# Small experts that add their row sums before the activation, a later transpose in the split experts, and norms that take their statistics from other operations

## What is computed

```python
def hier_moe(...):                      # first block, 32 experts of hidden width 256, 2 per token
    hg = silu(x @ w_gate[e]) * (x @ w_up[e])
    y += (hg * weight) @ w_down[e]
x = layer_norm(DN_ALPHA * x + y, ln2_g[layer], ln2_b[layer])

def second_block(x, ...):
    h = rmsnorm(x, norm_mix_w[l])       # l = 0 follows the last layer_norm above at once
    x = x + hybrid_mixer(h, ...)
    ...
    x = x + moe_swiglu(h, ...)          # second layer: 8 experts of hidden width 2816, 2 per token
```

## Time and profile before

| | |
|---|---|
| time, median of 3 runs (lowest, highest) | 2469.22 us (2465.05, 2471.34) |
| profiled execution: its time, and its span | 2465.34 us, 2463.3 us |
| mean granted TensorE clock | 0.983 of full |
| busy: PE, DVE, ACT | 94%, 72%, 56% of the span |
| weight traffic by SP's queue | 590.84 MB |

### The profile page before, as it was taken

How to read it: one execution, slowest core, us unless ns; L and a number is a source line. 1 busy time by engine, 2 the same in 40 slices (tenths; PEclk the granted TensorE clock), 3 DMA queues, 4 the chain that set the end, 5 groups by cost and what they waited for, 6 DMA issues and landing times.

```text
span 2463.3 us, 39708 instructions
## 1 busy us (share of the span) xinstructions
PE 2308.1 (94%) x14770; PEld 2068.1 (84%) x14770; DVE 1780.3 (72%) x2016; ACT 1378.1 (56%) x1522; POOL 70.2 (3%) x122
## 2 busy tenths in 40 slices
PE   7889999998899999988999998889999999999997
PEld 6789999877799998977899897778788887788876
DVE  5577775646777775885566688558888888888886
ACT  4455654445455653464433346437777777777775
POOL 0100000101000002000000200000000000000000
PEclk9999999999999999999999999989999999999999
DMA  7349999631399995634355652319899999998993
GB/s 266 127 151 364 366 374 327 171 107 51 113 359 375 376 353 127 211 101 135 120 181 170 160 183 91 132 36 361 324 331 390 337 357 374 329 390 330 338 394 116
DMA packets 253818, 609.51 MB, mean 247 GB/s; under 512 B 11217, under 2 KB 103201, under 8 KB 229009
## 3 DMA queue, kind: packets, MB, share of 16 engines
q1 hardware_dynamic: 247776, 590.84, 66.1%
q0 software_dynamic: 5248, 13.25, 2.4%
q10 hardware_dynamic: 560, 2.10, 0.2%
HBM read 605.11 MB, written 1.05 MB: 246 GB/s over the span
## 4 chain that ended last, share of the span: by engine, by line
PE 76%; DVE 13%; ACT 5%; issue 3%; DVEq 2%; DMA 1%; ACTq 0%; POOLq 0%
PE psum L137 15%; PE psum L139 15%; PE psum L138 15%; PE psum L2332 10%; PE psum L2368 9%; PE psum L2356 2%; DVE weight_ring_rounded L116 2%; DVE h_cf L3229 1%; ACT weights_high_rounded L2066 1%; PE psum L936 1%; ACT scores L970 1%; PE psum L2885 1%; PE psum L2015 1%; DVE weight_ring_rounded L2071 1%; PE psum L621 1%
## 5 line engine op out<-in xcount | busy, mean ns | idle before, releaser
L2071 DVE TENSOR_TENSOR weight_ring_rounded<-weight_ring,weights_high_rounded 128x2048 fp32r<-128x2048 f32 x264 | 603.7, 2291 | 101.5 <-ACT weights_high_rounded L2066 101.4
L2066 ACT ACTIVATE weights_high_rounded<-weight_ring 128x2048 fp32r<-128x2048 f32 x264 | 504.9, 1917 | 157.3 <-PE psum L139 142.9
L2429 DVE TENSOR_TENSOR weight_ring_rounded<-weight_ring,weights_high_rounded 128x2048 fp32r<-128x2048 f32 x128 | 293.0, 2292 | 96.8 <-ACT weights_high_rounded L2424 96.8
L137 PE MATMUL psum<-weights_high_rounded,scores_rounded 128*128 128x512 f32 (+1 forms) x768 | 291.2, 379 | 8.6 <-DVE weight_ring_rounded L2071 4.5
L139 PE MATMUL psum<-weights_high_rounded,scores_rounded 128*128 128x512 f32 (+1 forms) x768 | 287.0, 374 | 0.0
L138 PE MATMUL psum<-weight_ring_rounded,scores_rounded 128*128 128x512 f32 (+1 forms) x768 | 286.3, 373 | 0.0
L2332 PE MATMUL psum<-weights_high_rounded,scores_rounded 128*128 128x256 f32 x1024 | 262.6, 294 | 5.6 <-issue 3.3
L139 PE MATMUL psum<-weights_high_rounded,xT_rounded 128*128 128x512 f32 (+3 forms) x688 | 259.6, 377 | 0.0
L2332 PE MATMUL psum<-weight_ring_rounded,scores_rounded 128*128 128x256 f32 x1024 | 252.4, 284 | 0.0
L2368 PE MATMUL psum<-xT_high,weight_ring 128*128 128x128 f32 x2048 | 240.4, 276 | 7.3 <-DVE xT_high L2500 4.0
L2424 ACT ACTIVATE weights_high_rounded<-weight_ring 128x2048 fp32r<-128x2048 f32 x128 | 244.3, 1908 | 0.0
(11 more groups left out here) (580 smaller groups left out, 4123.5 us busy)
## 6 DMA issues: line engine op xcount, KB each, us to landing
weight_ring<-in_moe_w_gate_dram SPq DMA_DIRECT2D x152, 1024.0 KB, 6.0
weight_ring<-in_moe_w_up_dram SPq DMA_DIRECT2D x152, 1024.0 KB, 8.4
weight_ring<-in_moe_w_down_dram SPq DMA_DIRECT2D x152, 1024.0 KB, 8.3
weight_ring<-in_w_in_dram SPq DMA_DIRECT2D x20, 1024.0 KB, 7.2
weight_ring<-in_ffn_w_gate_dram SPq DMA_DIRECT2D x11, 1024.0 KB, 5.3
weight_ring<-in_ffn_w_up_dram SPq DMA_DIRECT2D x11, 1024.0 KB, 5.4
weight_ring<-in_ffn_w_down_dram SPq DMA_DIRECT2D x11, 1024.0 KB, 4.9
weight_ring<-in_w_out_dram SPq DMA_DIRECT2D x8, 1024.0 KB, 5.1
```

Of the source, the lines that this page charges most:

```text
L137: nc.tensor.matmul(out, lh, rh, start=start, stop=False)
L2066: self.c.nc.scalar.activation(ring.high(self.s0 + q, 1, SLOT), ring.view(self.p0 + q, 1, SLOT), ACT.Copy).then_inc(ring.high_ready, 1)
L2071: self.c.nc.vector.tensor_tensor(ring.low(self.p0 + q, 1, SLOT), ring.view(self.p0 + q, 1, SLOT), ring.high(self.s0 + q, 1, SLOT).bitcast( ...
L2429: self.c.nc.vector.tensor_tensor(ring.low(tile, 1, SLOT), ring.view(tile, 1, SLOT), ring.high(s, 1, SLOT).bitcast(F32), ALU.subtract).then ...
```

## The change

Four parts.

1. `SmallExperts`. ScalarE copies only the 64 low rows from PSUM, VectorE adds them to the 64 high rows, ScalarE takes the Silu of the sums (64x256), and VectorE multiplies (64x256), all in row form. TensorE then transposes the finished hidden rows, two transposes in place of four matmuls, and ScalarE copies them to `hidden`. The orders of ScalarE and VectorE change with it, and the result of expert x is written in step x, not in x+1. `e_twice` goes.
2. `SplitExpert`. In the last but one step `turn` stands behind the whole gate product, not in its middle, and at an expert's end VectorE makes the next window before it copies the rows. The tables that place the hidden copies on ScalarE and VectorE are written otherwise, and give these two the same order as before.
3. The two norms. The addition at the end of the last small experts also sums its row (`accum_out`); a small operation turns that into minus the mean. ScalarE squares x minus the mean and sums it, so the two statistics operations at 405 and 407 go. The RMSNorm that follows squares each block of rows as soon as that is normed, and the second block's gain product moves behind the variance. The idle products are 16, not 24.
4. In the first mixer two pairs of semaphores become one pair that counts to two; no instruction moves.

```diff
 class SmallExperts:
     def first(self, pe, x):
-            pe.wait_ge(*self.of(self.rows_taken, x - 2, 0))
+            pe.wait_ge(*self.of(self.rows_summed, x - 2, 0))
     def turn(self, pe, x):
-        pe.wait_ge(*self.of(self.rows_taken, x, 0))
+        pe.wait_ge(*self.of(self.rows_ready, x, 0))
...
-        blocks = self.rows[:, x % 2, :].rearrange("s (a f m) -> s a m f", a=2, m=2)
-        for a in range(2):
-            for m in range(2):
-                at = (2 * a + m) * self.W
-                last = nc.tensor.matmul(psum[:, 2 + x % 2, at:at + self.W], blocks[:, a, m, :], self.twice, start=True, stop=True)
+        blocks = self.hidden_rows.rearrange("s (f m) -> s m f", m=2)
+        for m in range(2):
+            last = self.c.nc.tensor.transpose(self.c.psum[:, 2 + x % 2, m * P:(m + 1) * P], blocks[:, m, :], self.c.ident[:, :])
...
     def scalar_step(self, act, x, i):
             act.wait_ge(*self.of(self.turned, x, i))
-            nc.scalar.activation(self.squashed, c.psum[:, 2 + x % 2, 0:2 * self.W].rearrange("p (m s) -> p m s", m=2),
-                                 ACT.Silu).then_inc(self.squash_done.sem, 1)
+            nc.scalar.activation(self.hidden[:, x % 2, :, 0:self.W], c.psum[:, 2 + x % 2, 0:2 * P].rearrange("p (m s) -> p m s", m=2)[:, :, 0:self.W],
+                                 ACT.Copy).then_inc(self.hidden_ready.sem, 1)
...
-            nc.scalar.activation(self.rows[:, (x + 1) % 2, :], c.psum[:, (x + 1) % 2, :], ACT.Copy).then_inc(self.rows_taken.sem, 1)
+            nc.scalar.activation(self.rows[0:self.W, (x + 1) % 2, :], c.psum[self.W:, (x + 1) % 2, :], ACT.Copy).then_inc(self.lows_taken.sem, 1)
         if x + 3 < n:
-            if x + 3 > 0:
-                self.high(act, x + 3, 0, i)
...
+            if x + 3 > 0:
+                self.high(act, x + 3, 0, i)
+        if 0 <= x + 1 < n:
+            act.wait_ge(*self.of(self.rows_summed, x + 1, i))
+            nc.scalar.activation(self.squashed_rows, self.rows[0:self.W, (x + 1) % 2, 0:CH], ACT.Silu).then_inc(self.squash_done.sem, 1)
     def vector_step(self, dve, x, i):
...
+        if 0 <= x + 1 < n:
+            rows = self.rows[0:self.W, (x + 1) % 2, :]
+            dve.wait_ge(*self.of(self.lows_taken, x + 1, i))
+            nc.vector.tensor_tensor(rows, c.psum[0:self.W, (x + 1) % 2, :], rows, ALU.add).then_inc(self.rows_summed.sem, 1)
...
+        if 0 <= x + 1 < n:
+            dve.wait_ge(*self.of(self.squash_done, x + 1, i))
+            nc.vector.tensor_tensor(self.hidden_rows[0:self.W, :], self.squashed_rows, self.rows[0:self.W, (x + 1) % 2, CH:],
+                                    ALU.mult).then_inc(self.rows_ready.sem, 1)
+        if 0 < x + 3 < n:
+            self.low(dve, x + 3, 0, i)
+        if x >= 0:
+            write(x)
 class SplitExpert:
-            first(self.gate(j + 1), j + 1, 0, lambda: turn(j))
             if j < steps - 2:
+                first(self.gate(j + 1), j + 1, 0, lambda: turn(j))
                 third(j)
                 first(self.up(j + 1), j + 1, 2)
             else:
+                first(self.gate(j + 1), j + 1, 0)
+                turn(j)
                 first(self.up(j + 1), j + 1, 2)
...
+        if next_window:
+            next_window()
         self.used(dve, self.p0 + self.down(self.steps - 1), i)
         nc.vector.tensor_copy(self.rows[:, 512:], c.psum[:, 5, :]).then_inc(self.rows_dve.sem, 1)
         if next_window:
-            next_window()
             self.low(dve, 1, i + 1)
 def sparse_experts(...):
+            nc.vector.scalar_tensor_tensor(c.x[:, t, :], c.x[:, t, :], alpha, made, ALU.mult, ALU.add, accum_out=means[:, t, :])
+            dve.drain()
+            nc.vector.tensor_scalar(means[:, t, :], means[:, t, :], -1.0 / D, None, ALU.mult).then_inc(*c.sig("chunk_added").up())
+def post_norm_by_sums(c, added):
...
+        for t in range(TT):
+            act.wait_ge(*added[t])
+            nc.scalar.activation(junk[:, t, :], c.x[:, t, :], ACT.Square, bias=less_mean[:, t, :], accum_out=c.stats[:, 0, t, 0:1])
...
+        for t in range(TT):
+            nc.vector.scalar_tensor_tensor(c.scaled[:, t, :], c.x[:, t, :], less_mean[:, t, :], c.gain[:, :], ALU.add, ALU.mult)
+        dve.wait_ge(*squared.at(1))
...
+def pre_norm_by_blocks(c, gain, idle, normed):
...
+        for t in range(TT):
+            act.wait_ge(*normed[t])
+            nc.scalar.activation(junk[t], c.x[:, t, :], ACT.Square, accum_out=c.stats[:, 0, t, 0:1])
...
+        nc.vector.tensor_tensor(c.scaled[:, 0, :], c.x[:, 0, :], gain, ALU.mult)
+        dve.wait_ge(*summed.at(1))
+        nc.vector.tensor_scalar(var, ss, 1.0 / D, RMS_EPS, ALU.mult, ALU.add).then_inc(*rooted.up())
+        nc.vector.tensor_tensor(c.scaled[:, 1, :], c.x[:, 1, :], gain, ALU.mult)
```

More of the change, by code:

```diff
@@ L2078, in order @@
         ups_done = {self.up(j) + self.tiles(j) - 1: j for j in range(self.steps)}
-        turns = {self.gate(j + 1) if j + 1 < last else self.gate(j + 1) - 1: j for j in range(last)}
+        turns = {self.gate(j + 1): j for j in range(last)}
         turns[self.down(last - 1)] = last
@@ L2085, in order @@
                 squash(squashes[q])
-            if q in turns and turns[q] != last - 1:
+            if q in turns:
                 part(turns[q])
@@ L2091, in order @@
                 next_split(0)
-            if q in turns and turns[q] == last - 1:
-                part(turns[q])
             if squash_first and q in squashes:
@@ L3066, in pre_norm, with _ @@
             column_steps(c, 0, c.scaled, c.xs, (4, 5, 6, 7), 0):
+        blocks[step.who](step.run)
+def post_norm_by_sums(c, added):
+    nc = c.nc
+    squared, rooted, done = c.sig("norm_stats"), c.sig("norm_rstd"), c.sig("rows_normed")
+    var, r, less_mean = c.var[:, 0, 0:TT, :], c.rstd[:, 0, 0:TT, :], c.stats[:, 1, 0:TT, 0:1]
+    landed = c.sig("norm_params_landed").now()
+    junk = c.psum[:, 0:4, :].rearrange("p (t a) b -> p t (a b)", t=TT)
+    @c.block.scalar
+    def _(act):
+        nc.scalar.activation(c.var[:, 3, 0, :], c.ones[:, 0:1], ACT.Sqrt)
+        for t in range(TT):
+            act.wait_ge(*added[t])
+            nc.scalar.activation(junk[:, t, :], c.x[:, t, :], ACT.Square, bias=less_mean[:, t, :], accum_out=c.stats[:, 0, t, 0:1])
+        act.drain().then_inc(*squared.up())
+        act.wait_ge(*rooted.at(1))
+        nc.scalar.activation(r, var, ACT.Sqrt).then_inc(*rooted.up())
+    @c.block.vector
+    def _(dve):
+        dve.wait_ge(*landed)
+        dve.drain()
+        for t in range(TT):
+            nc.vector.scalar_tensor_tensor(c.scaled[:, t, :], c.x[:, t, :], less_mean[:, t, :], c.gain[:, :], ALU.add, ALU.mult)
+        dve.wait_ge(*squared.at(1))
+        nc.vector.tensor_scalar(var, c.stats[:, 0, 0:TT, 0:1], 1.0 / D, LN_EPS, ALU.mult, ALU.add).then_inc(*rooted.up())
+        dve.wait_ge(*rooted.at(2))
+        inverse_root(c, r, var, c.newton[:, 0:TT, :])
+        for t in range(TT):
+            nc.vector.scalar_tensor_tensor(c.x[:, t, :], c.scaled[:, t, :], r[:, t, :], c.bias[:, :], ALU.mult, ALU.add).then_inc(*done.up())
@@ new lines, in pre_norm_by_blocks, with _ @@
+def pre_norm_by_blocks(c, gain, idle, normed):
+    nc, blocks = c.nc, {"pe": c.block.tensor, "act": c.block.scalar, "dve": c.block.vector}
+    summed, rooted, done = c.sig("squares_summed_0"), c.sig("rms_root_0"), c.sig("rms_diagonal_0")
+    ss, var, r = c.stats[:, 0, 0:TT, 0:1], c.var[:, 0, 0:TT, :], c.rstd[:, 0, 0:TT, :]
+    junk = [c.psum[:, a:a + 2, :].rearrange("p a b -> p (a b)") for a in (6, 0)]
+    landed = c.sig("gain_landed").now()
+    @c.block.tensor
+    def _(pe):
+        idle_products(c, pe, idle, 4)
+    @c.block.scalar
+    def _(act):
+        for t in range(TT):
+            act.wait_ge(*normed[t])
+            nc.scalar.activation(junk[t], c.x[:, t, :], ACT.Square, accum_out=c.stats[:, 0, t, 0:1])
+        act.drain().then_inc(*summed.up())
+        act.wait_ge(*rooted.at(1))
+        nc.scalar.activation(r, var, ACT.Sqrt).then_inc(*rooted.up())
+    @c.block.vector
+    def _(dve):
+        dve.wait_ge(*landed)
+        dve.drain()
+        nc.vector.tensor_tensor(c.scaled[:, 0, :], c.x[:, 0, :], gain, ALU.mult)
+        dve.wait_ge(*summed.at(1))
+        nc.vector.tensor_scalar(var, ss, 1.0 / D, RMS_EPS, ALU.mult, ALU.add).then_inc(*rooted.up())
+        nc.vector.tensor_tensor(c.scaled[:, 1, :], c.x[:, 1, :], gain, ALU.mult)
+        dve.wait_ge(*rooted.at(2))
+        inverse_root(c, r, var, c.newton[:, 0:TT, :])
+        for t in range(TT):
+            nc.vector.tensor_scalar(c.diag[:, 0, t, :], c.ident[:, :], r[:, t, :], None, ALU.mult)
+        dve.drain().then_inc(*done.up())
+    for step in column_steps(c, 0, c.scaled, c.xs, (4, 5, 6, 7), 0):
@@ L3766, in stages @@
                         mixed, taken = c.sig("chunk_added").now(), c.sig("slot_rows_low").now()
+                        added = [c.sig("chunk_added").at(t + 1) for t in range(TT)]
                         @c.block.gpsimd
@@ L3776, in _ @@
```

(3 more changed lines are left out.)

95 lines of the change are left out of this document (35 added, 60 removed).

## The result

The changed kernel takes 2444.25 us (median of 4 runs, 2438.0 to 2445.05) where the kernel before takes 2469.18: a ratio of 0.9906 with a 95% interval of 0.9894 to 0.9918, 23 us less by the ratio. The forecast was 2426.5 with a range of 2414 to 2444. Less than two thirds of the expected gain is there. The profiled execution took 2438.0 us (span 2435.9), 27.3 less than that of before.

The account below looks back on a forecast made before the run. TensorE was taken as the bound of the small experts, the DMA engines close behind. −39.6 + 3.4 − 2.0 + 7 − 8.5 − 3.0 = −42.7 from the profiled 2465.3 gave 2422.6, plus 3.9 to the median: 2426.5 us, range 2414 to 2444.

Parts of the forecast that it names:

- transposes for matmuls: Small experts, TensorE: two transposes replace four turning matmuls, 0.66 us less an expert, 19.8 a layer, −39.6 for two.
- cover of the chain: Small experts: the six hops ahead of `turn` stay hidden by `first` and `third`, 1.2 us to spare; cost zero.
- start of a layer: Expert 0: nothing hides the chain and its table load, so `third` starts 1.7 us late; +3.4 for two layers.
- end of a layer: Last `turn` to `third`: only two transposes and a copy remain, 0.7 us for 1.74; −1.0 a layer, −2.0.
- transfers: Small experts: weight tiles at 390 to 395 GB/s hold back the shorter step; +7 us, between 0 and +22.
- gaps ("small hitches"): Small experts: pieces sum to 8.33 of 8.55 us an expert, the rest called small hitches; no change was priced.
- split experts: TensorE's wait for VectorE's combination ahead of `turn` goes in all eight experts; −8.5 us, between −2 and −12.
- norms: Between the blocks: centring starts earlier and ScalarE squares beside it; −3.0 us, between −1.5 and −3.5.
- sign of being wrong: Small experts save less than 20 us over both layers, or split experts keep more than 4 of their 6.8.
- rival (a): Small experts: the DMA engines become the bound, 8.2 to 8.26 us an expert; 2438 to 2442 us, chance 0.22.
- rival (d): Start of a layer: TensorE's idle gap before the first `turn` lets the clock fall; +1.9 a layer, 2430, chance 0.05.
- the earlier window: Split experts' boundaries: VectorE's window ahead of the result's copy brings at most 4.1 us; −0.5 was taken.

Follow-up runs that it names:

- norms_only: The kernel before with only the norms between the blocks changed: 2462.3 us, ratio 0.9984 (0.9973 to 0.9996).

## Why the prediction was wrong, step by step

| step | forecast, us | measured, us | where it is read |
|---|---|---|---|
| transposes for matmuls | −39.6 | −40.8 | step 8.33 to 7.65, 60 experts |
| cover of the chain | 0 | 0 | no wait of `turn` within a layer |
| start of a layer | +3.4 | +7.2 | first product to second `turn`, the two kernels without branches |
| end of a layer | −2.0 | −2.0 | 1.74 to 0.76, each layer |
| transfers | +7 | 0 | 406 GB/s and no wait |
| gaps ("small hitches") | 0 | +21.8 | 12.1 to 33.9 in two layers |
| split experts | −8.5 | −8.5 | `turn(3)` to `turn(5)`, eight times |
| norms | −3.0 | −3.2 | 17.10 to 13.91 |
| sum | −42.7 | −25.5 | medians: −24.9 |

The step that failed is a half sentence in the first part: "together 8.33; the rest is small hitches". The hitches were in the window of the earlier trace rows, 4.3 us of standing still, and in the line of the earlier trace rows, "2.5 <-issue". I carried them over unchanged and asked neither what they were nor whether they depend on the pace. They were TensorE's sequencer waiting for its own instructions, and they grew from 12 to 34 us in two layers. With them priced at what was measured the forecast would have been 2448, and without the allowance for transfers 2441. Sum and forecast are 17.2 us apart: 21.8 for the gaps and 3.8 for the start, less 7 for the transfers and 1.4 for transposes and norms. So the allowance for transfers made the miss smaller by 7 us for a reason that did not hold, which is luck. The prediction's own sign of being wrong came: the small experts saved 13.8 us in the two layers, less than the 20 that it names.

**The transfers** were the wrong worry. I divided 362 GB/s by a busy share of 0.95 and took the 381 for what full engines can do. That quotient was not the limit here: with TensorE asking for more the same engines gave 406, at a share of 1.01. The row that told it was the one in the split experts, 406 in the earlier trace rows, and I should have trusted it. Curiously the changed kernel's own rate, 378 to 380 GB/s at a share of 0.97 to 0.98, looks just like rival (a): 3.15 MB at 381 GB/s are 8.26 us, and the mean expert took 8.21 to 8.25. The number fitted and the mechanism was another, as the kernels with fewer bytes and without branches showed.

**The start** was mis-sized by a factor of two, and what was missing is the prediction's rival (d), the clock. The layer's first product starts at 154.98 us before and at 157.01 after. Counted from there `turn(0)` was forecast at 11.9 us (166.9) and came at 12.1 (169.12); TensorE stood still 4.63 us ahead of it, and the forecast has 4.6 (162.3 to 166.9). That this fits is luck in part, since I left out of the chain the low part that stands ahead of the addition on VectorE (2.29 us). Behind it the forecast fails: `third(0)` came 3.91 us after `turn(0)`, where I had put 2.3. The granted clock was 0.68 over the 7 us from 169.5 on. A layer's start cost 3.6 us more than before, not 1.7; the 1.9 between them is the price that rival (d) had, with a chance of 0.05. (Its working is not in the earlier trace rows, though. At the lower level a matmul of the first product starts every 0.21 us, at 157.4 to 160.2, where it is 0.12 at full clock: 3.4 us for sixteen, not 3.84.) The timeline of the changed kernel's start, to set against the earlier trace rows:

```profile
163.98 2.29 DVE L2428 TENSOR_TENSOR weight_ring_rounded<-weight_ring,weights_high_rounded 128x2048 fp32r<-128x2048 f32 x1 [3.56 <-ACT weights_high_rounded L2423]
166.19 0.68 DVE L2507 TENSOR_TENSOR xT<-psum,xT 64x512 f32<-64x512 f32 x1
...
168.65 0.42 DVE L2515 TENSOR_TENSOR xT_high<-xT_high,xT 64x256 f32<-64x256 f32 x1 [1.19 <-ACT xT_high L2464]
```

```profile
166.91 1.28 ACT L2464 ACT_TABLE_LOAD   x1
```

The 7 us from 169.5 on, columns as in the earlier trace rows:

```profile
169.50:176.50 7.00, 7.00 (x45) 7.00 (x44) 5.25 (x4) 5.27 (x6) 0.00 (x0) 0.68 0.26 89
```

**What was right:** the 0.66 of the transposes, the chain's cover, the end of a layer, the norms, and the split experts as a whole. Within these one detail was off. I expected the earlier window to save 0.5 in all, at seven boundaries. The rows of the split experts after, to set against the earlier trace rows:

```profile
PE psum L137 <- issue: 4.3, 7, 0.7
PE psum L137 <- DVE weight_ring_rounded L2073: 3.6, 4, 1.1
PE psum L2056 <- DVE scores L2148: 3.1, 8, 0.4
```

The wait for the window (4.1, seven times) is gone, but seven waits of 4.3 us with no releaser stand at the same place. The two traces show why nothing was won. At the first boundary TensorE's sequencer goes through a branch, the loading of a count and another branch: from 1755.12 to 1756.31 before, where VectorE's window was done at 1756.19, and from 1734.70 to 1735.90 after. The first product starts 0.05 us behind it in both, at 1756.36 and 1735.96. The window had merely ended last but one. The other six stops are 0.5 to 0.7 us long in both kernels, as the first is. That the part came out at 8.5 as forecast is partly luck: 8.5 and 0 in place of 8.0 and 0.5.

## What to carry to other kernels

A wait that the profile calls "issue" on the engine that is the bound is a quantity like any other: look at the branches of its sequencer (shortest, median, longest), and if the longest is far above the median and under way when the engine stops, suspect that the engine waits for its own code; leave the branch out to see. Here code that is jumped over was fetched as well, and a branch for a rare case inside a tight stage cost more when the stage got faster; one branch for the whole stage took that away, and it was cheapest where the jump over the rare code fell into time in which the engine waited anyway. And do not take rate divided by busy share for the limit of the DMA engines (381 GB/s here, where 406 were reached); look for a stretch in which they are pressed.

## What was not expected of the hardware

- A test by TensorE's sequencer that goes on with the next code took 0.07 to 0.10 us. A jump over a body took 0.17 us at the least, up to 4.18 us over 32 matmuls and up to 2.52 over 16 in the changed kernel, and over twice as many up to 5.4 us. The jump over the general code of a whole layer took 5.9 and 6.2 us at the end of a stage and 3.7 and 3.3 at its start.
- Stops of about 2.2 us were followed once by a granted clock of 0.69 (205.35 us) and once by one of 1.00 (801.7 us) over the next `third`; the first cost 4.0 us, the second 2.4.
- The sequencer ran about 2.1 us ahead of TensorE ahead of `third`, and of the branch of 4.13 us at 203.05 only what went beyond that became a stop, 2.18 us.
- Tiles of 1 MB by one queue came at 406 GB/s over 220 us, beside TensorE busy all the time and VectorE and ScalarE busy 86% and 73%.
- The granted clock differed between kernels where the code is the same: 0.89 before and 1.00 after around the mixing, and from 47 to 52 us 1.00 before against 0.66 in the changed kernel and in `norms_only`; in both of these the operations behind it start 2 us later.
